# Other SBUF offsets for the matmul operands of a decoder block in split fp32

## The chip, the cores and the metric
One core of a Trainium2 chip. The metric is the device time of one execution in microseconds; of several runs the median is given.

## The reference
One decoder layer on 512 tokens of width 1024, all in float32. A combined projection gives u, v, q, k, values and two gates. Branch A is a causal spatial gating within chunks of 128 positions, branch B an attention with a window of 128 and a sink per head; both are projected, gated and merged, and a feed-forward part of width 4096 follows.
```python
h = rms_norm(x, norm_mix_pre)
proj = h @ w_in                                   # 1024 -> 5632
u, v_sgu, q, k, v_att, gate_a, gate_b = split(proj)
a = chunked_spatial_gating(gelu(u), gelu(v_sgu), ln_v_gain, ln_v_bias, w_spatial, b_spatial)
att = sliding_window_sink_attention(rotary(q), rotary(k), v_att, sinks)
merged = sigmoid(gate_a) * (a @ w_a) + sigmoid(gate_b) * (att @ w_b)
x = x + rms_norm(merged @ w_o, norm_mix_post)
ff = square(relu(rms_norm(x, norm_ff_pre) @ w_ff_in)) @ w_ff_out
out = x + rms_norm(ff, norm_ff_post)
```

## The kernel before
Each float32 operand of a large product is split into a rounded high part and the rest, both in the type fp32r, and a product is three matmuls (`product`, lines 1471 to 1476): high by high on line 1474, high by low on 1475, low by high on 1476. In all three the first operand is the one that is loaded into the array (a weight load of 128 columns of 4 bytes, 512 bytes of each partition), the second one moves through it (512 columns, 2048 bytes of each partition, or 256 columns).

The weights come in units of 1024 columns through a ring of four slots: `w_raw` is what the transfer brings, ScalarE rounds it into `w_hi`, VectorE subtracts for `w_lo`. The activations lie transposed in `actB_hi`/`actB_lo` (first the normalized input, later a, then the feed-forward input) and in `actA_hi`/`actA_lo` (q, then the attention's output, then the merged branches). Two forms of a unit share the ring:
- `columns_unit` (line 1478): the ring is loaded, the activations move, 8 x 3 matmuls. Used for the gates and u, for w_b, w_a and for the feed-forward's first product.
- `rows_step`, `rows_block` (lines 1486, 1495): the activations are loaded, the ring moves. Used for q, k, values, v, and w_o.

The down projection (`item_product`, line 1773) computes each 2 x 2 block of matrices with seven products in place of eight. There operands made of the activations are loaded: `op_hi`, with `op_lo` for three of the seven and `op_lo_sums` for the other four; the ring moves. The attention loads `actA` (q) and moves `kT` for the scores, and loads `v_pair` and moves `pT` for the values (lines 1625, 1626, 1651, 1654); TensorE also turns tiles by `ident` (lines 1516, 1608, 1635).

The order on every engine is written out by hand, with semaphores. The tensors lie in SBUF one behind the other as they are declared, at steps of 32 bytes. A group declared in its own `ExitStack` gives its place back, so the next group lies over it: `actA` and `op_hi`, `op_lo_sums` share region_a, and all that is declared after `r_denom` shares region_b, `op_lo` among it. `w_hi`, `w_lo`, `actB_hi`, `actB_lo`, `actA_hi`, `actA_lo`, `op_hi`, `op_lo_sums`, `w_raw`, `ident` and `mask` all have sizes that are multiples of 512 bytes. The 26 small tensors behind them, each filled up to 32 bytes, are 1920 bytes together, 3 x 512 + 384, so region_b begins 384 bytes above a multiple of 512 from the ring, which is 128 below the next one.

Of the kernel before, what the change touches and what calls it, by code (L numbers as in the profile page):

```python
# [36 lines left out]
F32 = mybir.dt.float32  # L37
F32R = mybir.dt.float32r
# [4 lines left out]
P = 128  # L43
D = 1024
S = 512
TT = S // P
KT = D // P
# [9 lines left out]
EPS = 1e-6  # L57
SCRATCH = 2048
ROOT_MEAN = D ** -0.5
NEG = -1e30  # L60
WARM_FIRST = 9
WARM_UP = 12
# [24 lines left out]
PAIRS = FF_UNITS // 2  # L87
# [195 lines left out]
def hybrid_block(nc, x, positions, w_in, ln_v_gain, ln_v_bias, w_spatial, b_spatial, sinks, w_a, w_b,  # L283
# [11 lines left out]
    with ExitStack() as ctx:  # L295
# [3 lines left out]
        def keep(name, shape, dt=F32):  # L299
            return ctx.enter_context(nc.sbuf_tensor(name, shape, dt))  # L300
# [3 lines left out]
        w_lo = keep("w_lo", [P, SLOTS, UNIT], F32R)  # L304


        actB_hi = keep("actB_hi", [P, KT, S], F32R)
        actB_lo = keep("actB_lo", [P, KT, S], F32R)
        def group(stack, spec):
            return [stack.enter_context(nc.sbuf_tensor(n, s, d)) for n, s, d in spec]  # L310

        with ExitStack() as a:
            actA_hi, actA_lo = group(a, [("actA_hi", [P, KT, S], F32R), ("actA_lo", [P, KT, S], F32R)])
        with ExitStack() as a:
            op_hi, op_lo_sums = group(a, [("op_hi", [P, PAIRS, 7, 2 * P], F32R),
                                          ("op_lo_sums", [P, PAIRS, 4, 2 * P], F32R)])
        ctx.enter_context(nc.sbuf_tensor("region_a", [P, PAIRS * 11 * 2 * P], F32))


        w_raw = keep("w_raw", [P, SLOTS, UNIT])  # L320
# [37 lines left out]
        with ExitStack() as a:  # L358
            x0, _, g_rows, g_hi, g_lo, pick, pick_r, _, qk = group(a, [
                ("x0", [P, TT, D], F32), ("pad0", [P, 4096], F32), ("g_rows", [P, G_COLS], F32),  # L360
                ("g_hi", [P, G_COLS], F32R), ("g_lo", [P, G_COLS], F32R), ("pick", [P, G_ROWS, P // 4], F32),
                ("pick_r", [P, G_ROWS, P], F32R), ("pad1", [P, 640], F32),
                ("qk", [P, TT, NH, HD], F32)])
            rot = [None] * 4
            rot[0], rot[1], rot[2], rot[3] = group(a, [(f"rot{i}", [P, TT, NQ, ROT], F32) for i in range(4)])
        with ExitStack() as a:
            v_sgu, ln_g, ln_b, b_s, w_s, _, w_mix = group(a, [
                ("v_sgu", [P, TT, D], F32), ("ln_g", [P, D], F32), ("ln_b", [P, D], F32),
                ("b_s", [P, GROUPS, P], F32), ("w_s", [P, GROUPS, P], F32),
                ("pad2", [P, 2 * KT, S], F32), ("w_mix", [P, GROUPS, P], F32)])  # L370
# [9 lines left out]
        with ExitStack() as a:  # L380
            _, mix = group(a, [("pad3", [P, 19456], F32), ("mix", [P, TT, D], F32)])
# [198 lines left out]
        def _(pool):  # L580
            steps = [0]

            def after(ins):

                steps[0] += 1
                ins.then_inc(pool_step, 1)
                pool.wait_ge(pool_step, steps[0])
# [22 lines left out]
            for i in range(ROT):  # L610
# [3 lines left out]

            after(nc.gpsimd.affine_select(out=mask[:], in_=mask[:], compare_op=ALU.is_gt, fill=NEG, base=0,
                                          pattern=[[1, 2 * P]], channel_multiplier=-1))
            nc.gpsimd.affine_select(out=mask[:], in_=mask[:], compare_op=ALU.is_ge, fill=NEG, base=P,
                                    pattern=[[-1, 2 * P]], channel_multiplier=1).then_inc(pool_consts, 1)
# [81 lines left out]
        def _(act):  # L700
# [27 lines left out]
            def square(t):  # L728
                act.wait_ge(x_in[t], 16)
                if t > 1:  # L730
                    act.wait_ge(ssq_act, t - 1)
                nc.scalar.activation(probs[:].rearrange("p h k -> p (h k)"), x0[:, t], ACT.Square, scale=ROOT_MEAN,
                                     accum_out=ssq[:, 0, t:t + 1]).then_inc(ssq_act, 1)
# [141 lines left out]
            def mix_square(part, t, src, signal):  # L875
                if part:
                    act.wait_ge(*part)
                nc.scalar.activation(junk_wo[:, 0:src.shape[1]], src, ACT.Square, scale=ROOT_MEAN,
                                     accum_out=ssq[:, t[0], t[1]:t[1] + 1]).then_inc(signal, 1)
# [51 lines left out]
            def ff_square(n, src, half, t):  # L931

                act.wait_ge(ff_ready, n + 1)
                if n:
                    act.wait_ge(ff_squared, n)
                nc.scalar.activation(ff_act[:, 0], src, ACT.Square, scale=ROOT_MEAN,
                                     accum_out=ssq[:, 4 + half, t:t + 1]).then_inc(ff_squared, 1)
# [909 lines left out]
```

## Time and profile before

| | us |
|---|---|
| median of 3 runs (lowest, highest) | 776.16 (775.42, 776.23) |
| the profiled execution | 775.11 |
| its span, first to last instruction | 773.4 |
| busy in it: TensorE matmuls | 763.0 |
| busy in it: weight loads | 640.4 |
| busy in it: VectorE | 531.8 |
| busy in it: ScalarE | 366.1 |

Matmuls overlap in the profile: a matmul is recorded from its start until its result is written, and the next one starts before that. So the distance between two starts is the pace, and the recorded duration is longer than it. A row of groups names the line, the engine, the tensor written, the tensors read, the shape, the count, and the mean duration in ns. Weight loads have rows of their own (PEld) with the line of their matmul.

### The profile page before, as it was taken

What the parts mean: (1) busy time and instruction counts of PE and PEld (TensorE: products, weight loads), DVE (VectorE), ACT (ScalarE), POOL (GpSimd) and SP (SyncE); (2) the same over time, 40 slices, a digit from 0 to 9 for tenths busy, and PEclk for the clock granted to TensorE, in tenths of its full rate; (3) what the DMA queues carried; (4) which work ended last, traced back from release to release, by engine and by line L of the source; (5) the groups of instructions that cost most, each with busy time, mean ns of one, the idle gap of its engine ahead of it and who ended that gap; (6) DMA issues with size and microseconds to landing.
All of it is one profiled execution on the core that took longest, in us unless ns stands there. A gap on an engine that the chain in (4) does not pass through costs nothing.

```text
span 773.4 us, 9929 instructions
## 1 busy us (share of the span) xinstructions
PE 763.0 (99%) x3633; PEld 640.4 (83%) x3633; DVE 531.8 (69%) x892; ACT 366.1 (47%) x612; POOL 63.1 (8%) x116
## 2 busy tenths in 40 slices
PE   8999999999999999999999999999999999999995
PEld 7888888888888888888888998888888888888884
DVE  6614587787777237885635769846885598659897
ACT  5522666665666743232325545543543345334442
POOL 3000000122232003000001200000000000000005
PEclk9999999999999999999999999999999999999999
DMA  7432132122212631426331453136102730163004
GB/s 269 136 112 82 56 108 82 56 82 81 84 56 82 196 103 59 127 61 245 108 109 55 164 174 125 36 126 235 39 1 82 251 103 1 54 215 112 0 1 109
DMA packets 92021, 80.82 MB, mean 105 GB/s; under 512 B 2885, under 2 KB 77641, under 8 KB 91977
## 3 DMA queue, kind: packets, MB, share of 16 engines
q1 hardware_dynamic: 91392, 79.19, 31.5%
q0 software_dynamic: 576, 1.05, 0.9%
q8 instruction: 27, 0.44, 0.2%
q14 instruction: 18, 0.14, 0.1%
q10 hardware_dynamic: 8, 0.00, 0.0%
HBM read 77.08 MB, written 3.15 MB: 104 GB/s over the span
## 4 chain that ended last, share of the span: by engine, by line
PE 92%; DVE 4%; POOL 1%; ACT 1%; issue 1%; DMA 0%; DVEq 0%; POOLq 0%
PE acc L1475 27%; PE acc L1474 27%; PE acc L1476 27%; DVE w_lo L1282 1%; PE aux L1476 1%; PE aux L1474 1%; PE aux L1475 1%; DVE sum L1305 1%; PE aux L1625 1%; PE aux L1626 1%; PE aux L1635 1%; PE aux L1700 1%; PE acc L1654 1%; PE acc L1651 1%; PE aux L1516 1%
## 5 line engine op out<-in xcount | busy, mean ns | idle before, releaser
L1474 PE MATMUL acc<-actB_hi,w_hi 128*128 128x512 f32 (+1 forms) x544 | 207.0, 380 | 0.0
L1476 PE MATMUL acc<-actB_hi,w_lo 128*128 128x512 f32 (+1 forms) x544 | 205.2, 377 | 0.0
L1475 PE MATMUL acc<-actB_lo,w_hi 128*128 128x512 f32 (+1 forms) x544 | 205.0, 377 | 0.0
L991 DVE TENSOR_TENSOR w_lo<-w_raw,w_hi 128x1024 fp32r<-128x1024 f32 x72 | 87.7, 1223 | 83.2 <-ACT w_hi L706 82.7
L1476 PEld LDWEIGHTS acc<-actB_hi,w_lo 128*128 128x128 f32 x544 | 102.4, 188 | 19.0
L1474 PEld LDWEIGHTS acc<-actB_hi,w_hi 128*128 128x128 f32 x544 | 102.4, 188 | 18.2
L1475 PEld LDWEIGHTS acc<-actB_lo,w_hi 128*128 128x128 f32 x544 | 102.5, 188 | 18.0
L706 ACT ACTIVATE w_hi<-w_raw 128x1024 fp32r<-128x1024 f32 x72 | 75.4, 1052 | 70.2 <-PE acc L1476 68.8
L1475 PE MATMUL acc<-w_lo,op_hi 128*128 128x512 f32 (+1 forms) x164 | 63.6, 388 | 0.0
L1474 PE MATMUL acc<-w_hi,op_hi 128*128 128x512 f32 (+1 forms) x164 | 63.0, 384 | 0.0
L1474 PE MATMUL acc<-w_hi,actB_hi 128*128 128x512 f32 x144 | 56.1, 390 | 0.0
L1476 PE MATMUL acc<-w_hi,actB_lo 128*128 128x512 f32 x144 | 56.0, 389 | 0.0
L1475 PE MATMUL acc<-w_lo,actB_hi 128*128 128x512 f32 x144 | 56.0, 389 | 0.0
L1282 DVE TENSOR_TENSOR w_lo<-down_raw,w_hi 128x1024 fp32r<-128x1024 f32 x32 | 39.0, 1223 | 16.1 <-ACT w_hi L918 16.1
L946 ACT ACTIVATE ff_act<-acc 128x512 f32<-128x512 f32 x32 | 19.1, 596 | 62.4 <-PE acc L1476 62.4
L918 ACT ACTIVATE w_hi<-down_raw 128x1024 fp32r<-128x1024 f32 x32 | 33.8, 1057 | 27.4 <-PE acc L1476 14.6
L1278 DVE TENSOR_TENSOR w_lo<-w_raw,w_hi 128x1024 fp32r<-128x1024 f32 x28 | 34.3, 1225 | 15.2 <-ACT w_hi L906 15.0
L817 ACT ACTIVATE probs<-scores_sb,neg_m 128x256 f32<-128x256 f32 (+1 forms) x64 | 30.1, 471 | 30.4 <-DVE sink_m L1149 30.4
L1321 DVE TENSOR_TENSOR ff_act<-ff_act 128x512 f32<-128x512 f32 x32 | 22.0, 689 | 25.9 <-ACT ff_act L946 25.8
L1476 PE MATMUL acc<-w_hi,op_lo 128*128 128x512 f32 (+1 forms) x100 | 38.8, 388 | 0.0
L906 ACT ACTIVATE w_hi<-w_raw 128x1024 fp32r<-128x1024 f32 x28 | 29.6, 1056 | 18.5 <-PE aux L1476 9.6
L1474 PEld LDWEIGHTS acc<-w_hi,op_hi 128*128 128x128 f32 x164 | 31.2, 190 | 6.9 <-issue 0.4
(215 smaller groups left out, 1341.9 us busy)
## 6 DMA issues: line engine op xcount, KB each, us to landing
w_raw<-in_w_in SPq DMA_DIRECT2D x44, 512.0 KB, 3.7
w_raw<-in_w_ff_in SPq DMA_DIRECT2D x32, 512.0 KB, 4.0
down_raw<-in_w_ff_out SPq DMA_DIRECT2D x16, 1024.0 KB, 6.2
w_raw<-in_w_b SPq DMA_DIRECT2D x8, 512.0 KB, 3.5
w_raw<-in_w_a SPq DMA_DIRECT2D x8, 512.0 KB, 3.5
w_raw<-in_w_o SPq DMA_DIRECT2D x8, 512.0 KB, 3.7
x<-in_x SPq DMA_DIRECT2D x4, 512.0 KB, 6.2
x<-in_x SPq DMA_DIRECT2D x1, 2048.0 KB, 9.6
```

The lines of the kernel that those rows point to most:

```text
L706: nc.scalar.activation(w_hi[:, j], w_raw[:, j], ACT.Copy).then_inc(hi_made, 1)
L817: nc.scalar.activation(probs[:, h, off:], scores_sb[:, h, off:], ACT.Exp, bias=neg_m[:, h:h + 1], accum_out=denom[:, h:h + 1])
L906: nc.scalar.activation(w_hi[:, r % SLOTS], w_raw[:, j], ACT.Copy).then_inc(hi_made, 1)
L918: nc.scalar.activation(moving(w_hi, r % SLOTS), right_raw(name, h), ACT.Copy).then_inc(hi_made, 1)
L946: nc.scalar.activation(ff_act[:, m % 4], acc[:, bank], ACT.Relu).then_inc(relu_made, 1)
L991: nc.vector.tensor_tensor(w_lo[:, j], w_raw[:, j], w_hi[:, j].bitcast(F32), ALU.subtract).then_inc(lo_made, 1)
L1278: nc.vector.tensor_tensor(w_lo[:, r % SLOTS], w_raw[:, up_slot(m)], w_hi[:, r % SLOTS].bitcast(F32), ALU.subtract).then_inc(lo_made, 1)
L1282: nc.vector.tensor_tensor(moving(w_lo, r % SLOTS), right_raw(PRODUCTS[k], h), moving(w_hi, r % SLOTS).bitcast(F32), ALU.subtract).then_inc ...
L1321: nc.vector.tensor_tensor(f, f, f, ALU.mult).then_inc(sq_made, 1)
L1474: nc.tensor.matmul(o, a_hi, b_hi, start=first, stop=False)
L1475: nc.tensor.matmul(o, a_hi, b_lo, start=False, stop=False)
L1476: return nc.tensor.matmul(o, a_lo, b_hi, start=False, stop=last)
```

## The change
Three empty tensors are declared: `step_acts` of 64 bytes before `actB_hi`, and, at the beginning of region_a, `step_a` of 192 bytes before `actA_hi` and `step_op` of 480 bytes before `op_hi`. region_a grows by the 480 bytes. Against the ring (`w_hi`, `w_lo`) and modulo 512 bytes, `actB` then lies at 64, `actA` at 64 + 192 = 256, `op_hi` and `op_lo_sums` at 64 + 480 - 512 = 32. All that is declared behind region_a moves up by 64 + 480 = 544 bytes: `w_raw` and `ident` from 0 to 32, region_b (`kT`, `v_pair`, `pT`, `probs`, `op_lo` and the rest) from 384 to 416, which is 96 below the next multiple. No instruction is added, removed or moved on any engine.
```diff
--- before.py
+++ after.py
@@ -57,6 +57,9 @@
 EPS = 1e-6
 SCRATCH = 2048
 ROOT_MEAN = D ** -0.5
+STEP_ACTS = 16
+STEP_A = 48
+STEP_OP = 120
 NEG = -1e30
 WARM_FIRST = 9
 WARM_UP = 12
@@ -304,17 +307,19 @@
         w_lo = keep("w_lo", [P, SLOTS, UNIT], F32R)
 
 
+        keep("step_acts", [P, STEP_ACTS])
         actB_hi = keep("actB_hi", [P, KT, S], F32R)
         actB_lo = keep("actB_lo", [P, KT, S], F32R)
         def group(stack, spec):
             return [stack.enter_context(nc.sbuf_tensor(n, s, d)) for n, s, d in spec]
 
         with ExitStack() as a:
-            actA_hi, actA_lo = group(a, [("actA_hi", [P, KT, S], F32R), ("actA_lo", [P, KT, S], F32R)])
+            _, actA_hi, actA_lo = group(a, [("step_a", [P, STEP_A], F32), ("actA_hi", [P, KT, S], F32R),
+                                            ("actA_lo", [P, KT, S], F32R)])
         with ExitStack() as a:
-            op_hi, op_lo_sums = group(a, [("op_hi", [P, PAIRS, 7, 2 * P], F32R),
+            _, op_hi, op_lo_sums = group(a, [("step_op", [P, STEP_OP], F32), ("op_hi", [P, PAIRS, 7, 2 * P], F32R),
                                           ("op_lo_sums", [P, PAIRS, 4, 2 * P], F32R)])
-        ctx.enter_context(nc.sbuf_tensor("region_a", [P, PAIRS * 11 * 2 * P], F32))
+        ctx.enter_context(nc.sbuf_tensor("region_a", [P, STEP_OP + PAIRS * 11 * 2 * P], F32))
 
 
         w_raw = keep("w_raw", [P, SLOTS, UNIT])
```

## Rows read from the trace of the kernel before

**Rows 1.** The page: busy time by engine, and the chain that ended last, by engine
```profile
PE 763.0 (99%) x3633; PEld 640.4 (83%) x3633; DVE 531.8 (69%) x892; ACT 366.1 (47%) x612; POOL 63.1 (8%) x116
...
PE 92%; DVE 4%; POOL 1%; ACT 1%; issue 1%; DMA 0%; DVEq 0%; POOLq 0%
```
**Rows 2.** The waits of TensorE: total us, times, longest
```profile
PE acc L1525 <- POOL ident L591: 1.7, 1, 1.7
PE acc L1542 <- ACT actB_hi L725: 0.3, 1, 0.3
PE acc L1530 <- DVE g_lo L1008: 0.2, 1, 0.2
```
**Rows 3.** The core's span and its mean granted TensorE clock
```profile
core 0: 773.4 us, clock 0.998
```
**Rows 4.** Timeline of PE, feed-forward's first product; columns: start us, duration us, instruction
```profile
477.73 0.39 PE L1476 MATMUL acc<-actB_hi,w_lo 128*128 128x512 f32 x1
...
480.45 0.39 PE L1476 MATMUL acc<-actB_hi,w_lo 128*128 128x512 f32 x1
```
**Rows 5.** Timeline of PE, one step's scores
```profile
137.02 0.29 PE L1625 MATMUL aux<-kT_hi,actA_hi 128*128 128x256 f32 x1
...
137.62 0.28 PE L1626 MATMUL aux<-kT_lo,actA_hi 128*128 128x256 f32 x1
137.75 0.28 PE L1625 MATMUL aux<-kT_hi,actA_lo 128*128 128x256 f32 x1
137.86 0.28 PE L1626 MATMUL aux<-kT_lo,actA_lo 128*128 128x256 f32 x1
137.98 0.38 PE L1635 MATMUL aux<-ident,probs 128*128 128x128 f32 x2
```
**Rows 6.** Groups of matmuls by form; columns: busy us, mean ns, idle us
```profile
L1476 PE MATMUL acc<-actB_hi,w_lo 128*128 128x512 f32 x480 | 187.1, 390 | 0.0
...
L1476 PE MATMUL acc<-w_hi,actB_lo 128*128 128x512 f32 x144 | 56.0, 389 | 0.0
...
L1476 PE MATMUL acc<-w_hi,op_lo 128*128 128x512 f32 x92 | 36.5, 397 | 0.0
...
L1476 PE MATMUL acc<-w_hi,op_lo_sums 128*128 128x512 f32 x64 | 24.9, 389 | 0.0
...
L1476 PE MATMUL acc<-actB_hi,w_lo 128*128 128x256 f32 x64 | 18.1, 283 | 0.0
...
L1700 PE MATMUL aux<-w_mix,v_sgu 128*128 128x128 f32 x64 | 7.8, 275 | 0.0
...
L1625 PE MATMUL aux<-kT_hi,actA_hi 128*128 128x256 f32 x24 | 6.9, 286 | 0.0
...
L1626 PE MATMUL aux<-kT_lo,actA_hi 128*128 128x256 f32 x24 | 6.8, 284 | 0.0
...
L1625 PE MATMUL aux<-kT_hi,actA_lo 128*128 128x256 f32 x24 | 6.8, 283 | 0.0
...
L1626 PE MATMUL aux<-kT_lo,actA_lo 128*128 128x256 f32 x24 | 6.8, 282 | 0.0
...
L1608 PE MATMUL aux<-ident,qk 128*128 128x128 f32 x40 | 5.0, 272 | 0.0
```
**Rows 7.** The weight loads' largest group, the same columns
```profile
L1476 PEld LDWEIGHTS acc<-actB_hi,w_lo 128*128 128x128 f32 x544 | 102.4, 188 | 19.0
```
**Rows 8.** Timeline of PE, first item of the down projection
```profile
480.68 0.39 PE L1474 MATMUL acc<-w_hi,op_hi 128*128 128x512 f32 x1
480.90 0.40 PE L1475 MATMUL acc<-w_lo,op_hi 128*128 128x512 f32 x1
...
486.22 0.39 PE L1474 MATMUL acc<-w_hi,op_hi 128*128 128x512 f32 x1
```
**Rows 9.** The page: VectorE's subtraction of a unit, and the loads of w_in
```profile
L991 DVE TENSOR_TENSOR w_lo<-w_raw,w_hi 128x1024 fp32r<-128x1024 f32 x72 | 87.7, 1223 | 83.2 <-ACT w_hi L706 82.7
...
w_raw<-in_w_in SPq DMA_DIRECT2D x44, 512.0 KB, 3.7
```

## The prediction, made before the changed kernel was run

> **What bounds the kernel now.** I read the page's busy shares first, then the chain of waits, then the waits of TensorE, and last the groups of matmuls by shape. TensorE (PE) is busy 763.0 of 773.4 us, VectorE 69%, ScalarE 47% [rows 1]. The chain that ended last lies 92% on PE and names the three lines of `product` [rows 1]. PE waits for others 2.2 us in the whole run, all of it near the start [rows 2]. The granted clock is 0.998 over the run [rows 3], the level of 2.4 GHz, so neither stalls nor the clock are to be won. What is left is the pace of the matmuls, and the change can work on that alone: every engine has the same instructions in the same order.
>
> **The pace, row by row.** A matmul's recorded duration is not its pace, since matmuls overlap. In the aligned stretch twelve of them start within 480.45 - 477.73 = 2.72 us, one each 226.7 ns, and each is recorded with 0.39 us [rows 4]. So duration less pace is 389 - 226.7 = about 163 ns, and the same 163 fits the 256-column form: eight starts in 137.98 - 137.02 = 0.96 us, 120 ns each, recorded with 282 to 286 [rows 5, 6]. I use that difference to read paces from mean durations.
>
> From 512 columns to 256 columns the pace falls by 226.7 - 120 = 106.7 ns, which is 256 columns at 2.4 GHz. So 512 columns take 213.3 ns, and **13.3 ns of each matmul do not depend on its length**. Each matmul has one weight load of 128 columns beside it [rows 7], so these 13.3 ns are a cost per weight load. There are 3020 matmuls of 512 columns. Each product is three, so a form's count in rows 6 stands for three times as many: 3 x 480 that move actB, 3 x 144 and 48 at the start that move the ring against a loaded actB, and from the loops of the code 192 and 192 the same two ways for actA (eight units of 24 each), 660 of the down projection (220 products) and 56 of the attention values. For them the fixed part is 3020 x 13.3 = 40 us, and this is what the change can reach.
>
> **Do offsets matter?** The kernel before already holds operands at three relations, and its rows can be read as experiments. Counting sizes from the start of the ring, w_hi, w_lo, actB, actA, op_hi, op_lo_sums and ident all stand at offset 0 within 512 bytes; the small tensors behind the mask add up to 1920 bytes, so all of region_b (kT, v_pair, pT, probs, v_sgu, w_mix, op_lo, the raw down weights) stands 128 bytes lower.
> - *All at the same offset*: 389 to 390 ns in almost every form, whichever tensors they are [rows 6]. Pace 226.7.
> - *One weight load in three at another offset* (op_lo, the others aligned): the triple is recorded with 0.39, 0.40, 0.40 us instead of three times 0.39, and 24 matmuls take 486.22 - 480.68 = 5.54 us, 230.8 each [rows 8]; the product of op_lo has 397 ns [rows 6]. The products of op_lo_sums, alike in all but the offset, stay at 389 [rows 6]. So an offset that changes from load to load costs about 4 ns per matmul.
> - *A standing distance* (scores: kT moves, actA is loaded, 128 bytes above it in every load): 286, 284, 283, 282 against 283 for the aligned 256-column form [rows 6]. The mean is the same; the single starts come 0.11 to 0.13 us apart [rows 5], so there is a beat with steps of some 3 ns up and down.
> - *Turning* (qk through ident, 128 bytes apart): 272, against 275 for w_mix and v_sgu, which are aligned with each other [rows 6]. As paces 109 against 112, and 109 is 2.4 ns above the 106.7 of 128 columns' weight load at half the array's rate.
>
> So the offset is a live quantity, of either sign, with rows from -3 ns to +7 ns. After the change the moving and the loaded operand are 64 bytes apart wherever actB takes part, 256 wherever actA does, 32 for op_hi and op_lo_sums, and 96 for op_lo (which still jumps by 128 against op_hi). None of these distances has a row of its own.
>
> **The sum.** The 56 matmuls of the values stay aligned with each other; 2964 of 512 columns change. Bounds on each: from -13.3 (all of the fixed part gone) to +7.3 (the worst of the triple, 397 - 389, as a pace 234 against 226.7). I take -3 ns, the nearest rows with a standing distance between the streams that show any gain: the low step of the scores' beat, and 109 against 112 in the turns. That gives 2964 x 3.0 = -8.9 us.
> The 192 matmuls of 256 columns on actB would add 192 x 3 ns = 0.6 us; I leave them to the range, since their beat may differ.
> The op_lo triples: 92 of 512 columns, 3 x 4 = 12 ns each over the aligned pace, 1.1 us in all; the jump stays 128, so 0.
> Loads and the other engines: w_raw moves from 0 to 32 bytes within 512 and region_b with it, so transfers and vector operations have other offsets too. A transfer of 512 KB lands in 3.7 us [rows 9], a unit of 24 matmuls takes 5.4 us, and PE waits for no load [rows 2]; cost 0, hidden by PE. If a landing doubled to 7.4 us, it would still find three other slots of work, 16 us, in front of it. VectorE's subtraction takes 1223 ns per unit [rows 9] against 5.4 us: also hidden. If PE becomes faster by 1 to 4% these two remain far from being the bound.
> Profiled execution: 775.11 - 8.9 = 766.2. It lies 1.05 us under the median of 776.16, so for a median I say **767**.
>
> A rule speaks against any effect. The Trainium skill, "TensorE: Matmul & The Clock Gate", section "Part 2: What happens when you issue a matmul", says that TensorE has two independent SBUF read ports and that loading the next weights steals no read bandwidth from the running matmul; "SBUF — State Buffer", section "Who interferes with whom", says that PE never waits on anyone. By these the sum would be 0. The trace disagrees for op_lo, where the same product costs 397 instead of 389.
>
> **Rivals.**
> 1. *Nothing changes* (within 0.2%, 1.55 us, or 0.5 ns per matmul, which is about what a measurement of this kernel can tell). For it: the mean over the scores' beat is exactly the aligned pace, as if every load met the moving stream a fixed number of times from whatever offset it starts. Against it: rows with 3 ns less and 4 ns more. 776.2. The skill's rule on the ports ends here as well. Chance 0.20.
> 2. *The fixed part is a meeting of two equal offsets and goes entirely*, down to the 2.4 ns that the turns leave: 13.3 - 2.4 = 10.9 ns x 2964 = -32.3 us, so 743.9 for a median. For it: the ring and nearly all operands are aligned, and the fixed part goes with the weight load. Against it: the scores, 128 apart, keep all of it. Chance 0.17. The skill's page on TensorE, section "Wait — 56ns, not 53.3ns?", gives columns / 2.4 + about 2.5 ns for back-to-back matmuls, 215.8 ns here; by that figure the gain would be an estimated 32 us too.
> 3. *Slower: standing distance costs what op_lo costs.* In the triple, a load 128 off the moving stream makes the matmul beside it and its own longer, by up to 8 ns. Place: all 2964; price: 4.1 ns on average as in the triple, +12.2 us, 788; with 7.3 ns each +21.6, 797. It decides from +0.5 ns per matmul. For it: the only long matmuls with a distance are slower. Against it: that distance jumps between loads, and after the change the distance stands still within each stage. Chance 0.30.
> That the change does not do what it says: the op group's distance is not uniform (op_lo), 100 of the 228 products there; this changes 1 us at most and has no chance of its own.
>
> **How the numbers follow.** A partial gain of about 3 ns (anything from 0.6 to 8 ns) has 0.33, and is likeliest; with rival 2, faster is 0.50. Same 0.20, slower 0.30. The range reaches down to rival 2 with a little beyond it, 742, and up to rival 3's average price with 1 us beyond it, 789; outside are the full 13.3 ns (737) and 7.3 ns on each (797). The likeliest case's own range is 753 to 775.
>
> **What would show it.** In the groups by form, the 128x512 products of actB should be recorded with about 386 instead of 389 ns, those of the down projection likewise, and the span should fall by the mean gain times 2964. Stages may differ, since they have different distances: if actB's forms fall and op's rise, both mechanisms act. The scores' distance becomes 160 and the values stay aligned, so the values should stay as they are. I am wrong if the forms stay at 389 (rival 1), fall to about 378 (rival 2), or rise to 393 and more (rival 3); wrong in another way if PE shows new waits for weights, which would mean that the loads suffered.

## The result, and the profile after

The changed kernel is slower: 783.59 us median (783.21 to 784.68, 4 runs) against 775.84 us (775.42 to 776.23, 4 runs), ratio 1.0103 with a 95% interval of 1.0092 to 1.0115. Its profiled execution took 783.46 us with a span of 781.7, 8.3 us more than the span of before.

From the page of the changed kernel: busy time by engine, the chain by engine, the loads of w_in.

```profile
PE 771.6 (99%) x3633; PEld 639.6 (82%) x3633; DVE 532.3 (68%) x892; ACT 366.4 (47%) x612; POOL 63.2 (8%) x116
...
PE 98%; DVE 0%; issue 0%; DMA 0%; ACT 0%; DVEq 0%; POOL 0%
...
w_raw<-in_w_in SPq DMA_DIRECT2D x44, 512.0 KB, 3.8
```

TensorE is busy 8.6 us more (763.0 before [rows 1]); the chain lies on it as before, and the loads land after 3.8 us instead of 3.7 [rows 9]. Its waits and the clock:

```profile
PE acc L1530 <- POOL ident L596: 1.8, 1, 1.8
PE acc L1547 <- ACT actB_hi L730: 0.3, 1, 0.3
PE acc L1535 <- DVE g_lo L1013: 0.3, 1, 0.3
```

```profile
core 0: 781.7 us, clock 0.997
```

The waits add up to 2.4 us against 2.2 [rows 2], the clock is 0.997 against 0.998 [rows 3]; even if all of that thousandth were lost time, it would be 0.8 us. So the 8 us are neither in waits nor in the clock; they are in the pace of the matmuls themselves. The groups of matmuls by form (busy us, mean ns, idle us; the lines of `product` are 1479 to 1481 now):

```profile
L1479 PE MATMUL acc<-actB_hi,w_hi 128*128 128x512 f32 x480 | 190.7, 397 | 0.0
L1481 PE MATMUL acc<-actB_hi,w_lo 128*128 128x512 f32 x480 | 188.2, 392 | 0.0
L1480 PE MATMUL acc<-actB_lo,w_hi 128*128 128x512 f32 x480 | 186.6, 389 | 0.0
...
L1481 PE MATMUL acc<-w_hi,actB_lo 128*128 128x512 f32 x144 | 56.9, 395 | 0.0
L1481 PE MATMUL acc<-w_hi,op_lo 128*128 128x512 f32 x92 | 36.4, 396 | 0.0
...
L1481 PE MATMUL aux<-w_hi,op_lo_sums 128*128 128x512 f32 x64 | 25.3, 396 | 0.0
...
L1480 PE MATMUL acc<-w_lo,actA_hi 128*128 128x512 f32 x64 | 24.9, 389 | 0.0
...
L1481 PE MATMUL acc<-actB_hi,w_lo 128*128 128x256 f32 x64 | 17.9, 279 | 0.0
...
L1659 PE MATMUL acc<-pT_lo,v_pair 128*128 128x512 f32 x28 | 11.1, 396 | 0.0
...
L1630 PE MATMUL aux<-kT_hi,actA_hi 128*128 128x256 f32 x24 | 6.7, 279 | 0.0
```

and, of the kernel before, two rows that are not among [rows 6]:

```profile
L1474 PE MATMUL acc<-actB_hi,w_hi 128*128 128x512 f32 x480 | 188.7, 393 | 0.0
...
L1475 PE MATMUL acc<-actB_lo,w_hi 128*128 128x512 f32 x480 | 186.9, 389 | 0.0
```

In a row the moving operand is named first and the loaded one second. A mean is still the pace plus about 163 ns. Read against [rows 6]: the ring against a loaded actB went from 389 to 395; op_lo_sums from 389 to 396; actB against a loaded ring has 397, 392, 389, where it had 393, 390, 389, so of a product's three matmuls, all at the same distance, the first lost 4 ns, one 2 and one nothing. The products with actA, 256 bytes off, stay at 389. The 256-column form of actB went down, from 283 to 279, and the scores' first from 286 to 279. The product with op_lo stays at 396 to 397, and the other matmuls of the down projection have come up to 395 and 396.

Busy times of the groups, added up, give the loss by stage; since two recorded durations overlap by the same amount before and after, a difference of busy times is a difference of time. The kernel before is taken by the same view:

| stage | matmuls | before us | after us | difference |
|---|---|---|---|---|
| actB moves, ring loaded (lines of `columns_unit`) | 1440 | 562.7 | 565.5 | +2.8 |
| ring moves, actB loaded | 432 | 168.1 | 170.8 | +2.7 |
| down projection, ring moves | 660 | 258.2 | 261.0 | +2.8 |
| actA, both ways | 384 | 150.0 | 150.1 | +0.1 |
| 256 columns: actB and scores | 288 | 81.8 | 81.0 | -0.8 |

That makes 7.6 us. The rest of the 8.3 us is the 48 first matmuls on actB, the values (each +0.2) and, for what is left, the start of the kernel.

### The profile page after: what moved, and what is told of

It is laid out like the page before. It is cut to its first block, busy times and chain, and to the rows that moved or that the text cites. A ratio compares the mean times of both kernels' runs of the same rounds, so it can differ in the third digit from the quotient of the medians.

```text
span 781.7 us, 9929 instructions
## 1 busy us (share of the span) xinstructions
PE 771.6 (99%) x3633; PEld 639.6 (82%) x3633; DVE 532.3 (68%) x892; ACT 366.4 (47%) x612; POOL 63.2 (8%) x116
## 4 chain that ended last, share of the span: by engine, by line
PE 98%; DVE 0%; issue 0%; DMA 0%; ACT 0%; DVEq 0%; POOL 0%
PE acc L1479 28%; PE acc L1481 28%; PE acc L1480 28%; PE aux L1481 2%; PE aux L1480 2%; PE aux L1479 2%; PE aux L1631 1%; PE aux L1630 1%; PE aux L1705 1%; PE aux L1640 1%; PE aux L1521 1%; PE acc L1659 1%; PE acc L1656 1%; PE aux L1613 1%; PE acc L1560 1%; PE acc L1547 1%
```

## The experiments

Distance below is the start of the moving operand less that of the loaded one, within 512 bytes. Every kernel is the one before with empty tensors put in; what lies behind a moved tensor is brought back to its place by further empty tensors (`step_raw` and the sizes of region_a do that), unless the text says otherwise. The diffs here show only the lines that set a distance; `...` stands for the others.

**Distance or place?** The first question was whether a matmul minds where its operands lie against each other, or where each of them lies. After the change pT and v_pair, which kept distance 0 from each other, had become slower (means 396 and 397 against 393 and 391 before), which spoke for place. So everything was moved, the ring too.

```diff
+        keep("step_all", [P, 8])
         w_hi = keep("w_hi", [P, SLOTS, UNIT], F32R)
```


> All tensors, the ring too, 32 bytes higher, so every distance between operands is as in the kernel before. The theory of distance (a matmul is slower when the loaded and the moving operand stand apart within 512 bytes) expects the time of before, 776 us, and 389 ns for the 128x512 products of actB. The theory of place (an operand is slower when its own start is no multiple of 128 bytes, whatever the other's) expects what pT and v_pair show after the change, where both lie 32 bytes past such a multiple: about 396 ns, +6 ns on each of some 3000 matmuls, about 793 us.

Measured: 775.49 us against 775.51, ratio 1.0003 (0.9993 to 1.0013). The groups by form:

```profile
L1477 PE MATMUL acc<-actB_hi,w_lo 128*128 128x512 f32 x480 | 187.4, 390 | 0.0
...
L1477 PE MATMUL acc<-w_hi,actB_lo 128*128 128x512 f32 x144 | 56.1, 390 | 0.0
...
L1655 PE MATMUL acc<-pT_lo,v_pair 128*128 128x512 f32 x28 | 11.0, 393 | 0.0
```

All are where they were, within a nanosecond. That is what distance expects, and not what place expects (396 ns, 793 us). With `[P, 16]` in that line, 64 bytes:

> All tensors 64 bytes higher, every distance as before. Distance expects 776 us. Place, if the step that matters is 64 bytes, expects 776 us too; if it is 128 bytes, 780 to 793 us, with the rows of actB slower by 2 to 6 ns as after the change, where actB lies 64 past a multiple of 128.

Measured: 775.05 us, one run. Place is out, for moves of 32 and 64 bytes. The first of them also shows that the places of w_raw and region_b as such cost nothing: they lie there as after the change, 32 bytes higher within 512 than before, and the transfers and the vector operations did not slow the kernel. Their distance from the ring is another matter; after the change it differs, here it does not. The two partial kernels below, which leave w_raw and region_b where they were, account for the whole loss without it.

**Which part of the change costs.** actB alone:

```diff
+        keep("step_acts", [P, 16])
         actB_hi = keep("actB_hi", [P, KT, S], F32R)
...
```


> Only actB is moved, by 64 bytes, all others keep their places. Both theories expect what the stages of actB show after the change: columns (actB moves) +2 ns, rows (actB is loaded) +6 ns, so 1440 x 2 + 480 x 6 = 5.8 us, 781.5 us; the down projection and the values at their old pace, 389 ns outside op_lo.

Measured: 780.81 us, ratio 1.0072 (1.0055 to 1.0088), +5.3 us where 5.8 were expected. By busy time actB's moved form costs 3.0 us more than before and its loaded form 2.4:

```profile
L1475 PE MATMUL acc<-actB_hi,w_hi 128*128 128x512 f32 x480 | 190.4, 397 | 0.0
L1477 PE MATMUL acc<-actB_hi,w_lo 128*128 128x512 f32 x480 | 188.4, 393 | 0.0
L1476 PE MATMUL acc<-actB_lo,w_hi 128*128 128x512 f32 x480 | 186.9, 389 | 0.0
...
L1477 PE MATMUL acc<-w_hi,actB_lo 128*128 128x512 f32 x144 | 56.8, 394 | 0.0
...
L1477 PE MATMUL aux<-w_hi,op_lo_sums 128*128 128x512 f32 x64 | 24.9, 389 | 0.0
...
L1477 PE MATMUL acc<-actB_hi,w_lo 128*128 128x256 f32 x64 | 17.7, 277 | 0.0
```

The down projection's group is back at 389. The 256-column form is at 277 here and at 279 after the change, with the same distance of 64. Then op alone:

```diff
-            op_hi, op_lo_sums = group(a, [("op_hi", [P, PAIRS, 7, 2 * P], F32R),
+            _, op_hi, op_lo_sums = group(a, [("step_op", [P, 8], F32), ("op_hi", [P, PAIRS, 7, 2 * P], F32R),
...
```


> Only op_hi and op_lo_sums 32 bytes higher, all others in the places of before. Distance expects what the down projection shows after the change, 233.3 ns for each of its 660 matmuls against 228.9: +2.9 us, 778.4 us, ratio 1.0037, which with the 5.3 us of actB alone makes up the whole loss. If the loss of the down projection came from w_raw or region_b at other places, it would be 775.5 here.

Measured: 777.90 us, ratio 1.0032 (1.0020 to 1.0044), +2.5 us. The two parts add up to 7.8 us; the whole change measures 7.8 (783.59 - 775.84). actA's 256 bytes, w_raw and region_b are left with nothing, within the intervals of these runs.

**Or the writes into the ring?** Moving actB or op_hi changes one more distance: ScalarE and VectorE write `w_hi` and `w_lo` while TensorE reads. If those writes were in the way, a matmul beside one would be slower than a matmul without. The starts in the trace of the changed kernel say no. From 525 to 567 us (actB moves) three matmuls in a row take 228.9 ns each in the 101 cases where such a write runs and 228.9 in the 82 where none does; from 20 to 80 us (actB loaded) it is 233.3 in the 144 cases and 233.4 in the 113.

**All distances.** Three kernels hold several distances at once, one per stage, and are read by their groups rather than by their time.

```diff
+        keep("step_acts", [P, 32])
...
+            _, actA_hi, actA_lo = group(a, [("step_a", [P, 112], F32), ("actA_hi", [P, KT, S], F32R), ("actA_lo", [P, KT, S], F32R)])
...
+            _, op_hi, op_lo_sums = group(a, [("step_op", [P, 32], F32), ("op_hi", [P, PAIRS, 7, 2 * P], F32R),
...
+        keep("step_b", [P, 32])
```


> actB at 128 from the ring, actA at 64, op_hi and op_lo_sums at 256, region_b (op_lo, kT, pT, v_pair) at 0. Distance expects slower actB and op forms by 2 to 6 ns. Place (128 bytes) expects 389 ns for actB, op and pT, and slower forms only for actA: +2 ns where it moves, +6 ns where it is loaded. Place in steps of 64 expects 389 ns for all.

Measured: 785.48 us, one run.

```profile
L1478 PE MATMUL acc<-actB_lo,w_hi 128*128 128x512 f32 x480 | 189.6, 395 | 0.0
...
L1479 PE MATMUL acc<-w_hi,actB_lo 128*128 128x512 f32 x144 | 56.9, 395 | 0.0
...
L1479 PE MATMUL acc<-w_hi,op_lo 128*128 128x512 f32 x92 | 35.9, 390 | 0.0
...
L1478 PE MATMUL acc<-w_lo,actA_hi 128*128 128x512 f32 x64 | 25.2, 394 | 0.0
```

actB at 128 is slow both ways (395), actA at 64 too (394), and op at 256 is as fast as at 0 (390), op_lo included, although op_lo and op_hi are 256 apart here. So 256 counts like 0. Neither theory had all of it: place had expected 389 for actB, and distance had expected op to be slower.

```diff
+        keep("step_acts", [P, 8])
...
+            _, actA_hi, actA_lo = group(a, [("step_a", [P, 16], F32), ("actA_hi", [P, KT, S], F32R), ("actA_lo", [P, KT, S], F32R)])
...
+            _, op_hi, op_lo_sums = group(a, [("step_op", [P, 32], F32), ("op_hi", [P, PAIRS, 7, 2 * P], F32R),
...
+        keep("step_b", [P, 72])
```


> Distances not tried so far: actB 32 bytes above the ring, actA 96, op_hi, op_lo and op_lo_sums 160, region_b also 160. If every distance that is no multiple of 256 costs, all of these forms are 2 to 7 ns slower per matmul of 512 columns. If there is a distance at which the loaded and the moving operand miss each other, one of them falls under 386 ns (under 224 in pace), down to 378 (216).

Measured: 791.37 us, one run, the slowest of all.

```profile
L1478 PE MATMUL acc<-actB_lo,w_hi 128*128 128x512 f32 x480 | 189.6, 395 | 0.0
...
L1479 PE MATMUL acc<-w_hi,actB_lo 128*128 128x512 f32 x144 | 57.0, 396 | 0.0
...
L1478 PE MATMUL acc<-w_lo,actA_hi 128*128 128x512 f32 x64 | 25.4, 396 | 0.0
...
L1479 PE MATMUL aux<-w_hi,op_lo_sums 128*128 128x512 f32 x64 | 25.1, 392 | 0.0
...
L1479 PE MATMUL acc<-actB_hi,w_lo 128*128 128x256 f32 x64 | 17.9, 279 | 0.0
```

No group of 512 columns falls under 389; none of these distances is better than 0. The 256-column form is at 279 again.

Tensors are laid out at steps of 32 bytes, so for smaller distances the operands start inside larger tensors:

```diff
+        actB_hi = inside(keep("actB_hi", [P, KT * S + 128], F32R), 4, KT * S).rearrange("p (k s) -> p k s", s=S)
+        actB_lo = inside(keep("actB_lo", [P, KT * S + 128], F32R), 4, KT * S).rearrange("p (k s) -> p k s", s=S)
...
+            actA_hi, actA_lo = (inside(t, 2, KT * S).rearrange("p (k s) -> p k s", s=S) for t in (actA_hi, actA_lo))
```


> actB 16 bytes above the ring and actA 8 bytes (the allocator gives 32 at the least, so the tensors are larger and the operands start inside them); the down projection's operands at 256 and region_b at 256. The distance theory in steps of 32 expects actB and actA at the aligned pace of 226.7 ns; if the distance counts byte by byte, they are slower by 2 to 7 ns like 32. op at 256 with op_lo at 256 too: 226.7 for all its 660.

Measured: 781.61 us, one run.

```profile
L1481 PE MATMUL acc<-actB_lo,w_hi 128*128 128x512 f32 x480 | 189.2, 394 | 0.0
...
L1482 PE MATMUL acc<-w_hi,actB_lo 128*128 128x512 f32 x144 | 56.2, 390 | 0.0
L1482 PE MATMUL acc<-w_hi,op_lo 128*128 128x512 f32 x92 | 35.9, 390 | 0.0
...
L1481 PE MATMUL acc<-actA_lo,w_hi 128*128 128x512 f32 x64 | 25.3, 395 | 0.0
...
L1482 PE MATMUL acc<-w_hi,actA_lo 128*128 128x512 f32 x64 | 25.1, 393 | 0.0
```

Sixteen and eight bytes are enough to be slower, 394 and 395 where the activations move; where they are loaded it is 390 and 393. So the distance counts in steps smaller than 32 bytes. The down projection, with all its operands at 256, is at 389 and 390 throughout, as expected.

The mean of 390 hides something. The groups where actB is loaded, taken in three stretches (25 to 79, 251.5 to 273 and 275.5 to 296 us of this kernel):

```profile
L1482 PE MATMUL acc<-w_hi,actB_lo 128*128 128x512 f32 x80 | 31.1, 389 | 0.0
...
L1482 PE MATMUL acc<-w_hi,actB_lo 128*128 128x512 f32 x31 | 12.2, 394 | 0.0
...
L1482 PE MATMUL acc<-w_hi,actB_lo 128*128 128x512 f32 x31 | 12.1, 389 | 0.0
```

The same operands at the same distance run at the aligned pace in two stretches and 5 ns slower in one; by the starts it is 226.7, 233.3 and 226.7 ns. And where actA moves at 64 bytes (mix1), one of a product's three matmuls, in the stretch before the matmuls of `w_mix` and `v_sgu` begin (299 to 320.4 us) and in the one where they come in between (323.6 to 349.5 us):

```profile
L1478 PE MATMUL acc<-actA_lo,w_hi 128*128 128x512 f32 x31 | 12.3, 398 | 0.0
...
L1478 PE MATMUL acc<-actA_lo,w_hi 128*128 128x512 f32 x30 | 11.7, 389 | 0.0
```

By the starts the pace is 233.3 ns in the first stretch and about 229 in the second, which is the pace of actB at 64 after the change (228.9). So away from 0 and 256 a distance does not fix the pace by itself: it allows more than one, and which one runs is decided by something else, perhaps by what ran before; no run singles it out.

From the recorded durations in the traces, each form's average over the three matmuls of a product less the same form's before (op from its three groups that write aux, in which no op_lo takes part). They are averages over whole stages, and by the rows above a stage can hold two paces:

| distance mod 256 | stage, kernel | ns per matmul of 512 columns |
|---|---|---|
| 0 | op in mix1 (256); actB moves in by256 (256, below) | +0.5; -0.1 |
| 8 | actA moves, sub32 | +5.2 |
| 16 | actB moves, sub32 | +4.5 |
| 32 | actB moves, sweep1 | +5.4 |
| 64 | actB moves, after and actb64; actA moves, mix1 | +2.0, +2.1; +5.3 (two paces) |
| 96 | actA moves, sweep1; op, sweep1 | +5.2; +6.0 |
| 128 | actB, mix1, moved; loaded | +5.5; +6.0 |
| 160 | actA loaded, sweep1 | +7.1 |
| 192 | actB loaded, after; actA loaded, mix1 | +6.1; +5.2 |
| 224 | op, after; actB loaded, sweep1 | +6.5; +6.4 |
| 240 | actB loaded, sub32 | +1.4 (0 in two stretches, about +6.6 in one) |
| 248 | actA loaded, sub32 | +3.7 |

No distance is faster than 0, and 0 (with 256) is the only one at which every stage is fast. The distances below 96 were tried only with the activations moving and those above 128 only with them loaded, so the table does not tell the distance from the role.

**The repair.** If so, the kernel before has one thing left to mend: region_b, 128 bytes off.

```diff
+        keep("step_b", [P, 32])
```


> The kernel before with 128 empty bytes ahead of region_b, so op_lo, kT, pT and v_pair also stand at distance 0 from the ring and from actA. The theory that any distance but a multiple of 256 costs, and distance 0 does not, expects the op_lo product at 389 instead of 397 ns and its neighbour at 389 instead of 396, 92 triples x 12 ns = 1.1 us, and less at the turns to and from the attention's products, some 14 x 15 ns = 0.2 us: 774.2 us against 775.5, ratio 0.998. The rival, that op_lo is slow because it lies in the high part of SBUF, expects 397 ns again and no change.

Measured: 774.09 us against 775.41, ratio 0.9983 (0.9974 to 0.9992), 11 runs. It is faster than the kernel before by the 1.3 us that were expected, and than the changed one by 9.5.

```profile
L1476 PE MATMUL acc<-w_lo,op_hi 128*128 128x512 f32 x156 | 60.7, 389 | 0.0
...
L1477 PE MATMUL acc<-w_hi,op_lo 128*128 128x512 f32 x92 | 35.8, 389 | 0.0
...
L1652 PE MATMUL acc<-pT_hi,v_pair 128*128 128x512 f32 x28 | 10.9, 389 | 0.0
L1655 PE MATMUL acc<-pT_lo,v_pair 128*128 128x512 f32 x28 | 10.9, 389 | 0.0
...
L1609 PE MATMUL aux<-ident,qk 128*128 128x128 f32 x40 | 5.0, 272 | 0.0
```

op_lo is at 389 (397 before [rows 6]), the values at 389 both. op_lo lies as high in SBUF as before, within 128 bytes, so its slowness had been its distance, or the jump of the distance from load to load, which is gone with it. The turning of qk, at distance 0 here and at 128 before, has 272 both times [rows 6].

```diff
+        keep("step_acts", [P, 64])
...
+            _, actA_hi, actA_lo = group(a, [("step_a", [P, 64], F32), ("actA_hi", [P, KT, S], F32R), ("actA_lo", [P, KT, S], F32R)])
...
+        keep("step_b", [P, 32])
```


> actB, op_hi and op_lo_sums at 256 from the ring, actA and region_b at 0. If the distance counts modulo 256, all forms of 512 columns are at 389 ns and the time is that of the aligned kernel, 774.1 us, ratio 0.998. If it counts modulo 512, actB's and op's products are slower by 2 to 7 ns, 780 us or more. The jump of 256 between op_hi and op_lo should cost nothing under the first.

Measured: 774.55 us, ratio 0.9987 (0.9977 to 0.9996); its interval and that of the aligned kernel overlap. 256 counts as 0 for every operand, and 128 does not, so I take the period as 256 bytes.

```profile
L1479 PE MATMUL acc<-w_hi,actB_lo 128*128 128x512 f32 x144 | 56.0, 389 | 0.0
...
L1479 PE MATMUL acc<-w_hi,op_lo 128*128 128x512 f32 x92 | 35.8, 389 | 0.0
```

**Why the values slowed.** pT and v_pair kept distance 0 from each other. I expected that they inherit something from the slow products of actB before them.

```diff
+        keep("step_b", [P, 8])
```


> Only region_b 32 bytes higher (96 instead of 128 below the ring), as after the change, with actB, actA and op aligned. After the change the products of pT and v_pair became 4 ns slower although they kept distance 0 from each other. If they inherit a state from the matmuls of actB before them, they are as in the kernel before here (230.2 ns on average, 227 between pT_lo and the next pT_hi). If their own new place against the ring does it, 234 and 233. The op_lo triple stays slow, 3 to 7 ns per matmul. Time 775 to 776 us.

Measured: 775.41 us, one run. The first of the two expectations fell: actB is aligned here, and the values are slower than before all the same. This kernel, then the kernel before, then mix1:

```profile
L1655 PE MATMUL acc<-pT_lo,v_pair 128*128 128x512 f32 x28 | 11.1, 396 | 0.0
L1652 PE MATMUL acc<-pT_hi,v_pair 128*128 128x512 f32 x28 | 11.0, 393 | 0.0
```

```profile
L1654 PE MATMUL acc<-pT_lo,v_pair 128*128 128x512 f32 x28 | 11.0, 393 | 0.0
L1651 PE MATMUL acc<-pT_hi,v_pair 128*128 128x512 f32 x28 | 11.0, 391 | 0.0
```

```profile
L1657 PE MATMUL acc<-pT_lo,v_pair 128*128 128x512 f32 x28 | 11.1, 395 | 0.0
L1654 PE MATMUL acc<-pT_hi,v_pair 128*128 128x512 f32 x28 | 11.0, 393 | 0.0
```

Moving region_b alone gives 3 of the 4 ns that the values lost after the change. Each step has two or four values' matmuls behind a stretch of actB. By the starts in the traces the first three take 230.9, 228.3 and 226.0 ns before (a jump of 128 bytes from the ring to region_b), 229.3, 232.8 and 235.9 in this kernel (a jump of 96), and 226.8, 226.6 and 226.7 in the aligned one (no jump). In mix1 the values lie at distance 0 from each other and from the ring, and the actB before them is 128 off (the scores' actA 64); they are at 395 and 393 too. So a matmul's pace depends on more than its own two operands: a jump at the border is enough to slow some matmuls behind it (this kernel), and so, it seems, is a stage off distance 0 before it (mix1). I have no run that shows what carries this over.

## Why the prediction was wrong

- *The number*: 767 us was forecast, 783.59 measured, a loss of 7.75 us instead of a gain of 8.9. It lies inside the range of 742 to 789 only because the range was drawn up to rival 3; the forecast itself had the wrong sign.
- *What bounds the kernel*: right. Waits, clock, loads and the other engines hardly moved (0.2 us of waits, a thousandth of clock), and of the 8.3 us in span about 8 are pace of matmuls.
- *"So the offset is a live quantity, of either sign"*: half right. For matmuls of 512 columns it has one sign. Clear negative differences occur for 256 columns alone (283 to 277 and 279), on 288 matmuls, worth 0.8 us after the change.
- *"I take -3 ns, the nearest rows with a standing distance"*: this is the step that failed. The term stood at -3.0 ns on 2964 matmuls; it measured +2.9 on average (8.6 us of busy time over 2964). 2580 of them (1440 and 480 of actB, 660 of the down projection) got slower, by 2.0, 6.1 and 4.2 ns on average. The two rows behind the -3 did not show a gain from distance at all. The turns: in the aligned kernel ident and qk stand at distance 0, and the row is the same 272 as at 128, so 109 against 112 ns is a difference between two forms, not between two distances. The scores: in the aligned kernel, at distance 0, they have 280, 283, 283, 283, where they had 286, 284, 283, 282 at 128, so distance had cost them 1.5 ns on average. And both rows are short forms, whose length hardly sets their pace: 128 columns take 109 to 112 ns, 256 take 120 and 512 take 226.7 [rows 4, 5, 6]. They were poor witnesses for 512 columns. The only rows of 512 columns with a distance between operands, op_lo's 397 and its neighbour's, said +4 ns on average over the triple, and I set them aside because there the distance jumps. Standing distances cost 2.0 to 6.5 ns after the change.
- *"The mean is the same"*, which I read from the scores for the rival of no change: near, but for 256 columns at 128 bytes alone (284 against 282 on average).
- *Bounds*: -13.3 to +7.3 held every form as an average over a product's three matmuls, the upper one closely (+7.1 at 160); single groups of the sweep rose further, `w_lo,op_hi` from 389 to 399. The range's lower part was empty: its end rested on rival 2, that the 13.3 ns are a meeting of equal offsets. In no kernel did a group of 512 columns come under 389, at eleven distances besides 0, so for 512 columns the fixed part is not that and stays unexplained.
- *Rival 3* named the mechanism and the sign. Its size, +12.2 us, was too large for this change because it priced all matmuls alike: actA's 384 got 256 bytes, which count as 0 (+0.1 us instead of 1.6), and actB's 1440 moved ones, the largest group, lost the least of all that were off (+2.8 us instead of 5.9). With these two at their measured prices the rival's sum would be 12.2 - 1.5 - 3.1 = 7.6 us. That it comes so near is in part luck: actB's loaded form was priced too low (4.1 instead of 6.1), and the short forms' 0.8 us were not in it.
- *Cost 0 for w_raw, region_b and the other engines*: right, within the intervals. In all32 they lie as after the change and the time is that of before, and actb64 and op32 make up the loss with them in their old places.
- *"the jump stays 128, so 0"* for op_lo: its product stayed at 396, but op_hi's own distance made all three of the triple slow, and the jump can no longer be told apart.
- *The rules of the Trainium skill*, that loading the next weights steals no read bandwidth from the running matmul ("TensorE: Matmul & The Clock Gate", Part 2) and that PE never waits on anyone ("SBUF — State Buffer", "Who interferes with whom"), had given a sum of 0. Moving actB alone by 64 bytes costs 5.3 us, and moving everything by 64 or 32 bytes costs nothing (775.05 and 775.49 us). The measurement decides: where the loaded and the moving operand lie against each other does matter here, with 4-byte operands. That the two reads get in each other's way is the nearest explanation, and it is not shown; no row shows a wait of TensorE on it.

## What to carry to other kernels

In a kernel bound by matmuls whose loaded and moving operands are both 4-byte tensors in SBUF, let both start at the same offset modulo 256 bytes, for all tensors that are used one after the other; in the kernels here other offsets cost 2.5 to 16 us of 776, and a last 128 empty bytes won 1.3 us. Small tensors declared between large ones spoil it silently, so declare the large ones first or fill up behind the small ones. And a row bears only on its own form, and only if something compares like with like: the -3 ns came from two different forms of 128 columns, and nothing showed that their distance made the difference.

## What the runs showed of the hardware that I had not expected

- The pace of a 512-column matmul depends on the distance between the start of its moving and of its loaded operand, with 256 counting as 0, and 8 bytes already matter: 226.7 ns at 0, up to 7 ns more on average elsewhere. Moving both by 32 or 64 bytes does not matter (775.49 and 775.05 against 775.51 us).
- Away from 0 one distance has more than one pace: at 240 bytes 226.7 ns in two stretches and 233.3 in a third of the same kernel, at 64 bytes 233.3 and 229 in one stage of mix1. At distance 0 the 512-column matmuls have one pace, 226.7 ns, in every stage, once a jump is over. What chooses among them elsewhere is open.
- The sign turns for 256 columns: actB's second and third matmul of a product take 283 at distance 0, 277 to 280 at 16, 32 and 64, and 284 at 128.
- About 13 ns per matmul, by the difference of the 512- and 256-column forms at distance 0, do not depend on the length. Each matmul has one weight load beside it, but no run shows that the load is their cause; for 256 columns at 64 bytes about 6 of them go (283 to 277).
